# Sparse attention in a hybrid decoder layer: the last 16 queries' index scores packed over heads, the value up-projection in 64-column products, table loads issued by SyncE, weights split in quarters

## What is computed

```python
# index scores: 8 heads of 64, one key for all heads
score = einsum("bqh,bqhs->bqs", wb, relu(einsum("bqhd,bsd->bqhs", qib, ki)))
_, idx = top_k(score, 128)                # among the keys not later than the query
logits = einsum("bqhc,bqkc->bhqk", qb, kv_sel) + bias      # 16 heads, latent width 128
o_lat = einsum("bhqk,bqkc->bqhc", softmax(logits), kv_sel)
o = einsum("bthc,hcd->bthd", o_lat, w_dsa_uv)              # value up-projection, 64 columns a head
```

## Time and profile before

| | us |
|---|---|
| Median of the runs (1400.37 to 1403.15) | 1402.95 |
| Profiled execution, its own time | 1399.39 |
| Its span on the core | 1397.6 |
| TensorE busy | 1331.5 (95%) |
| POOL busy | 791.4 (57%) |
| VectorE busy | 646.8 (46%) |
| ScalarE busy | 389.9 (28%) |

### The profile page before, as it was taken

The page is one execution under the profiler, slowest core; times in us unless marked ns, Lnnn a source line. Parts: engine busy times, 40 slices in busy tenths (PEclk is TensorE's granted clock), DMA queues, the critical chain, the costliest instruction groups (busy, mean ns, idle before and its releaser), DMA issues.

```text
span 1397.6 us, 17236 instructions
## 1 busy us (share of the span) xinstructions
PE 1331.5 (95%) x6467; PEld 1049.4 (75%) x6467; DVE 646.8 (46%) x1111; ACT 389.9 (28%) x789; POOL 791.4 (57%) x919
## 2 busy tenths in 40 slices
PE   6999999989999999999999889999989999999997
PEld 4866787656898778677887567678868888888886
DVE  3248896832246747542365655334252111333334
ACT  4244444443013232333022331331331111211322
POOL 8457433102663544555763553478477777888882
PEclk9999999999999999999999999999989999999999
DMA  6863222101321212222332331252223333222221
GB/s 180 207 218 98 61 61 70 32 22 41 96 76 46 76 46 61 61 61 64 102 85 76 91 91 28 72 181 94 73 80 101 91 91 107 96 99 91 91 91 60
DMA packets 168521, 121.08 MB, mean 87 GB/s; under 512 B 12345, under 2 KB 146591, under 8 KB 168439
## 3 DMA queue, kind: packets, MB, share of 16 engines
q1 hardware_dynamic: 161142, 108.30, 26.5%
q10 hardware_dynamic: 7296, 11.69, 2.8%
HBM read 115.72 MB, written 9.62 MB: 90 GB/s over the span
## 4 chain that ended last, share of the span: by engine, by line
PE 85%; DVE 8%; ACT 3%; issue 2%; ACTq 1%; DMA 0%; DVEq 0%; SPq 0%
PE GP L1671 41%; PE PA L1707 8%; PE GP L1707 6%; PE GP L1686 6%; PE GP L1668 4%; PE PA L1906 3%; PE GP L1857 2%; PE PA L1814 2%; PE PA L1904 1%; PE PA L1837 1%; PE PA L1893 1%; PE PA L1793 1%; PE PA L1870 1%; DVE hres L1596 1%; DVE xn L1595 1%
## 5 line engine op out<-in xcount | busy, mean ns | idle before, releaser
L588 POOL TENSOR_TENSOR wlo<-wraw,whi 128x256 fp32r<-128x256 f32 x712 | 587.0, 854 | 14.8
L584 POOL TENSOR_SCALAR whi<-wraw 128x1024 fp32r<-128x1024 f32 x178 | 195.0, 1096 | 538.1 <-PE GP L1671 319.4
L1671 PE MATMUL GP<-xh,whi 128*128 128x512 f32 x368 | 154.8, 421 | 2.6 <-DVE xl L1151 1.4
L1671 PE MATMUL GP<-xl,whi 128*128 128x512 f32 x368 | 147.7, 401 | 0.0
L1671 PE MATMUL GP<-xh,wlo 128*128 128x512 f32 x368 | 147.7, 401 | 0.0
L1624 DVE TENSOR_TENSOR ul<-U,uh 128x512 fp32r<-128x512 f32 x64 | 65.3, 1058 | 106.8 <-ACT uh L1081 106.8
L1671 PE MATMUL GP<-nh,whi 128*128 128x512 f32 x256 | 102.3, 400 | 0.7 <-DVE nl L1608 0.7
L1671 PE MATMUL GP<-nl,whi 128*128 128x512 f32 x256 | 102.1, 399 | 0.0
L1671 PE MATMUL GP<-nh,wlo 128*128 128x512 f32 x256 | 102.0, 398 | 0.0
L1628 DVE TENSOR_TENSOR U<-U 128x512 f32<-128x512 f32 x32 | 34.6, 1080 | 144.9 <-ACT U L1085 144.9
L1671 PEld LDWEIGHTS GP<-xh,whi 128*128 128x128 f32 x368 | 70.8, 192 | 21.9 <-issue 3.1
(11 more groups left out here) (345 smaller groups left out, 2772.4 us busy)
## 6 DMA issues: line engine op xcount, KB each, us to landing
wraw<-in_w_in SPq DMA_DIRECT2D x75, 512.0 KB, 3.7
wraw<-in_w_up SPq DMA_DIRECT2D x32, 512.0 KB, 4.0
wraw<-in_w_down SPq DMA_DIRECT2D x32, 512.0 KB, 3.5
line_rows<-bias_line SPq DMA_DIRECT2D x1, 5240.0 KB, 26.2
table<-line_rows SPq DMA_DIRECT2D x1, 4096.0 KB, 14.5
wraw<-in_w_br_dsa SPq DMA_DIRECT2D x8, 512.0 KB, 4.7
wraw<-in_w_br_gla SPq DMA_DIRECT2D x8, 512.0 KB, 3.9
wraw<-in_w_br_ml SPq DMA_DIRECT2D x8, 512.0 KB, 4.0
```

The lines of the kernel that those rows point to most:

```text
L584: nc.gpsimd.tensor_scalar(hi, src, 1.0, 1.0, ALU.mult, ALU.mult).then_inc(hi_done, 1)
L588: part = nc.gpsimd.tensor_tensor(lo[:, at:to], src[:, at:to], hi[:, at:to].bitcast(FP32), ALU.subtract)
L1671: ins = mm(ps[0:t.m, 0:SEQ], wt[:, s0, w], av, start=st, stop=sp_)
```

## The change

- The last tile's eight score steps go. The 16 queries of the eight heads are packed in one block of 128 columns (q4, block diagonal over the two halves of 64 rows), one product gives 128 rows (head, query) by 528 keys; VectorE applies relu and the head's weight in one operation, and a product with a 0/1 matrix (selT) adds the heads up. Small operations before the steps prepare the weights by row (wcol) and selT; POOL clears q4.
- SCORE_FILL is rewritten for 24 steps, the query tiles follow after single steps from v = 10 to 14. Between the packed product and the sum stands uq0.
- Eight fewer top-k items are done beside the steps; `rest` has 52 items instead of 44, and `ranked_after` gives two a group up to g = 19, then four in three groups.
- The first half of gb2 moves from group 0 to before the loop.
- The 16 table4 loads and the uvp load move to SyncE, ahead of the load of yb5's chunk, each behind its wait. uvp has 64 columns a head, is not cleared, and comes in one DMA.
- The up-projection writes each head's 64 columns as a product of its own, the first to PSUM partitions 0 to 63, the second to 64 to 127.
- POOL's first pass over a chunk is split in four of 256 columns, as the second is.

```diff
-SCORE_FILL = {1: ["uq4"], 3: ["uq5"], 5: ["uq6"], 7: ["uq7"], 9: ["uq8", "mo0"], 11: ["uq9"], 13: ["uq10"], 15: ["uq11"],
-              17: ["uq12", "mo1"], 19: ["uq13"], 21: ["uq14"], 23: ["uq15"], 25: ["mo2"], 29: ["mo3"]}
+SCORE_FILL = {1: ["uq4"], 3: ["uq5"], 5: ["uq6"], 7: ["uq7"], 9: ["uq8", "mo0"], 10: ["uq9"], 11: ["uq10"], 12: ["uq11"],
+              13: ["uq12"], 14: ["uq13"], 15: ["uq14", "mo1"], 17: ["uq15"], 19: ["mo2"], 21: ["mo3"]}
+LAST_QUERIES = [0, 1, 2, 3]
 GROUP_FILL = ["gb2", "gb3", "gb4", "gb5", "gb6", "gb7", "mo4", "mo5", "mo6", "mo7"]
...
             query(int(name[2:])) if name[:2] == "uq" else gate(name)
-    for h in range(4):
+    for h in LAST_QUERIES:
         query(h)
...
         SO = QO + DSA_H * SEQ * 4
-        (uvp,) = region(SO, [("uvp", [P, DSA_H, P], FP32)])
+        (uvp,) = region(SO, [("uvp", [P, DSA_H, 64], FP32)])
...
         hold_out, ld_mo, mo_sig = sem("hold_out"), sem("ld_mo"), sem("mo_sig")
+        q4_zero, q4i_ok, wc_ps, sc_w, s4_ok = sem("q4_zero"), sem("q4i_ok"), sem("wc_ps"), sem("sc_w"), sem("s4_ok")
         q4_ok, tail_in, gb_sig = sem("q4_ok"), sem("tail_in"), sem("gb_sig")
...
         pt_ps, pt_a, pt_d, pv_ps, ol_ev = sem("pt_ps"), sem("pt_a"), sem("pt_d"), sem("pv_ps"), sem("ol_ev")
-        uv_zero, ld_uv, uv_ps, yh_b, yl_b = sem("uv_zero"), sem("ld_uv"), sem("uv_ps"), sem("yh_b"), sem("yl_b")
+        ld_uv, uv_ps, yh_b, yl_b = sem("ld_uv"), sem("uv_ps"), sem("yh_b"), sem("yl_b")
         ld_a, gla_c, gg_a, gg_l, G_ok = sem("ld_a"), sem("gla_consts"), sem("gg_a"), sem("gg_l"), sem("G_ok")
...
         ROUNDS = TOPK // 8 + 1
+        STEPS = (QT - 1) * IDX_H
+        hmask, hpick, wcol, selT = psm[:, 0:IDX_H], low[:, 0:IDX_H], low[:, IDX_H:IDX_H + 1], prec[:, 0:META]
         WIO = 960
+        WCO = 1000
         GROUPS = QT * NHEADS2 + 1
...
                     sp.wait_ge(split_done, c["r"] - NRAW + 1)
+                if c is chunks[tl["yb5"].chunks[0]]:
+
+                    sp.wait_ge(lg_mn, 3 * DSA_H + 3)
+                    for h_ in range(DSA_H):
+                        sp.dma_start(table4[META * (h_ % 8):META * (h_ % 8 + 1), h_ // 8, :],
+                                     bass.AP(tensor=scratch.tensor, offset=h_ * LPITCH + META - 1,
+                                             ap=[[DSA_H * LPITCH - 1, META], [1, ALL]])).then_inc(tail_in, 16)
+                    sp.wait_ge(keep_ok, QT)
+                    sp.dma_start(uvp[:, :, :], a["w_dsa_uv"][0].rearrange("h c d -> c h d")).then_inc(ld_uv, 16)
...
             nc.gpsimd.memset(lm[:, :, :], 1.0).then_inc(pool_c, 1)
+            nc.gpsimd.memset(q4[:, :, :], 0.0).then_inc(q4_zero, 1)
             pool.wait_ge(pool_c, 7)
...
                                   ident[0:META, 0:META].unsqueeze(1).broadcast_to([META, IDX_H, META])).then_inc(masks, 1)
+            pool.wait_ge(q4_zero, 1)
+            nc.gpsimd.tensor_copy(q4[0:META, 1, :].rearrange("p (h q) -> p h q", q=META),
+                                  ident[0:META, 0:META].unsqueeze(1).broadcast_to([META, IDX_H, META])).then_inc(q4_zero, 1)
             pool.wait_ge(masks, 3 + len(LEVELS))
...
                 src, hi, lo = wraw[:, c["raw"], 0:n], whi[:, c["hl"], 0:n], wlo[:, c["hl"], 0:n]
-                if c is chunks[tl["yb4"].chunks[0]]:
-
-                    pool.wait_ge(keep_ok, QT)
-                    nc.gpsimd.memset(uvp[:, :, :], 0.0).then_inc(uv_zero, 1)
                 pool.wait_ge(raw_in[c["raw"]], c["load"])
...
                     pool.wait_ge(gemm_done, c["after"])
-                nc.gpsimd.tensor_scalar(hi, src, 1.0, 1.0, ALU.mult, ALU.mult).then_inc(hi_done, 1)
+                for at in range(0, n, PIECE):
+                    to = min(at + PIECE, n)
+                    part = nc.gpsimd.tensor_scalar(hi[:, at:to], src[:, at:to], 1.0, 1.0, ALU.mult, ALU.mult)
+                part.then_inc(hi_done, 1)
                 pool.wait_ge(hi_done, c["r"] + 1)
...
                 nc.scalar.activation(qi[:, m, :], ready(f"iq{m}")[:, 0:SEQ], ACT.Copy, scale=0.125).then_inc(gfree[tl[f"iq{m}"].slot], 1)
-            for v in range(QT * IDX_H):
+            act.wait_ge(q4_zero, 2)
+            for m in range(4):
+                whole(f"iq{m}")
+            for e in range(2):
+                r = slice(64 * e, 64 * e + 64)
+                nc.scalar.activation(q4[r, 0, r].rearrange("p (m q) -> p m q", q=META), qi[r, :, TILE_AT[QT]:SEQ], ACT.Copy).then_inc(q4i_ok, 1)
+            for v in range(STEPS):
                 r, w = TILE_ROWS[1 + v // IDX_H], TILE_KEYS[1 + v // IDX_H]
...
                         hold_away(int(name[2:]))
-            act.wait_ge(sc_ps, QT * IDX_H)
-            for h in range(4):
+            act.wait_ge(sc_ps, STEPS + 2)
+            nc.scalar.activation(S[0:META, QT - 1, :], PA[1][0:META, 0:ALL], ACT.Copy).then_inc(s4_ok, 1)
+            act.wait_ge(q4i_ok, 2)
+            for h in LAST_QUERIES:
                 query(h)
...
                                          ACT.Copy).then_inc(ol_ev, 1)
-                if g == 3 * NHEADS2 + 1:
-
-                    act.wait_ge(lg_mn, 3 * DSA_H + 3)
-                    for h_ in range(DSA_H):
-                        act.dma_start(table4[META * (h_ % 8):META * (h_ % 8 + 1), h_ // 8, :],
-                                      bass.AP(tensor=scratch.tensor, offset=h_ * LPITCH + META - 1,
-                                              ap=[[DSA_H * LPITCH - 1, META], [1, ALL]])).then_inc(tail_in, 16)
-                if g == TAIL - 2:
-                    act.wait_ge(uv_zero, 1)
-                    act.dma_start(uvp[:, 0::2, 0:64], a["w_dsa_uv"][0, 0::2].rearrange("h c d -> c h d")).then_inc(ld_uv, 16)
-                    act.dma_start(uvp[:, 1::2, 64:P], a["w_dsa_uv"][0, 1::2].rearrange("h c d -> c h d")).then_inc(ld_uv, 16)
             for m in range(KT):
...
                     if r == 0:
+                        if i == QT:
+                            dve.wait_ge(s4_ok, 1)
                         seq(tt(S[0:n_, i - 1, own], S[0:n_, i - 1, own], later_neg[0:n_, META:META + n_], ALU.add))
...
-            beside = [(1, r) for r in range(ROUNDS)] + [(2, r) for r in range((QT - 1) * IDX_H - ROUNDS)]
-            for v in range(QT * IDX_H):
+            per_head = ident[:, :].rearrange("p (g q) -> p g q", q=META)
+            nc.vector.tensor_reduce(hmask, per_head, mybir.AxisListType.X, ALU.add)
+            seq(nc.vector.tensor_reduce(selT, per_head.rearrange("p g q -> p q g"), mybir.AxisListType.X, ALU.add))
+            dve.wait_ge(wc_ps, 1)
+            seq(tt(hpick, PA[1][:, WCO:WCO + IDX_H], hmask, ALU.mult))
+            seq(nc.vector.tensor_reduce(wcol, hpick, mybir.AxisListType.X, ALU.add))
+
+            ahead = STEPS - IDX_H
+            for v in range(STEPS):
                 i, h = 1 + v // IDX_H, v % IDX_H
...
                 if v >= IDX_H:
-                    tile_, r = beside[v - IDX_H]
-                    dve.wait_ge(sc_acc, tile_ * IDX_H)
-                    topk(tile_, [r])
-            dve.wait_ge(sc_acc, QT * IDX_H)
+                    dve.wait_ge(sc_acc, IDX_H)
+                    topk(1, [v - IDX_H])
+            dve.wait_ge(sc_acc, STEPS)
+            dve.wait_ge(sc_ps, STEPS + 1)
+            ts(rl[:, 0, :], PA[0][:, 0:ALL], 0.0, wcol, ALU.max, ALU.mult).then_inc(sc_w, 1)
             dve.wait_ge(table_in, 16)
...
-            rest = [(2, r) for r in range((QT - 1) * IDX_H - ROUNDS, ROUNDS)] + [(t, r) for t in (3, 4) for r in range(ROUNDS)]
+            rest = [(1, r) for r in range(ahead, ROUNDS)] + [(t, r) for t in (2, 3, 4) for r in range(ROUNDS)]
...
-                return 2 * g if g < 16 else 32 + g - 16
+                return 2 * g if g < 20 else 40 + (g - 20) * 4 // 3
...
                 evacuated(f"iq{m}")
-            for v in range(QT * IDX_H):
+            pe.wait_ge(q4_zero, 2)
+            mm(PA[1][:, WCO:WCO + IDX_H], q4[0:META, 1, :],
+               wi[0:META, QT - 1, :].rearrange("p (m e) -> p e m", e=2), start=True, stop=True).then_inc(wc_ps, 1)
+            for v in range(STEPS):
                 i, h = 1 + v // IDX_H, v % IDX_H
...
                     gemm(name)
-            for h in range(4):
+            pe.wait_ge(q4i_ok, 2)
+            pe.wait_ge(sc_rl, STEPS - 1)
+            for c in (slice(0, SEQ), slice(SEQ, ALL)):
+                ins = mm(PA[0][:, c], q4[:, 0, :], kn[:, c], start=True, stop=True)
+            ins.then_inc(sc_ps, 1)
+            gemm(f"uq{LAST_QUERIES[0]}")
+            pe.wait_ge(sc_w, 1)
+            pe.wait_ge(sc_rl, STEPS)
+            for c in (slice(0, SEQ), slice(SEQ, ALL)):
+                ins = mm(PA[1][0:META, c], selT, rl[:, 0, c], start=True, stop=True)
+            ins.then_inc(sc_ps, 1)
+
+            for h in LAST_QUERIES[1:]:
                 gemm(f"uq{h}")
-
             evacuated(*[f"uq{h}" for h in range(DSA_H)])
-            pe.wait_ge(sc_rl, QT * IDX_H)
             pe.wait_ge(masks, 3 + len(LEVELS))
...
                 logits(v)
```

(8 more changed lines are left out.)

## The result

The changed kernel takes 1377.76 us (median of 4 runs, 1375.82 to 1380.14) against 1401.66 for the kernel before in the same session: a ratio of 0.983 (95% interval 0.9808 to 0.9853), 23.9 us less. The forecast was 14.9 less, 1388.0, and its range ended at 1381. The sign was right, the size was not, and the profiles say where. The profiled execution of after took 1379.02 us, with a span of 1377.1.

The account below looks back on a forecast made before the run. The prediction took TensorE's queue of matrix products to bound the kernel (85% of the span). Its terms summed to -14.9 us, 1384.5 for the profiled execution's kind and 1388.0 for the median, range 1381 to 1397.

Parts of the forecast that it names:

- Split in quarters: POOL's first pass, all 178 chunks: shorter holds of VectorE outweigh POOL's added time, net -2.0 us, bounds +2 to -5.
- Score stage: Packed last-tile scores: eight steps saved, but extra visits, end waits and the selT sum cost more, +1.2 us.
- Start of the loop: Attention loop start: half of gb2 fills TensorE's softmax wait (-1.0) and the half-clock dip goes (-1.5).
- Table loads: Attention group 25: TensorE's stall behind ScalarE's DMA issues goes, -8.2 us; uvp issues leaving ScalarE, -0.3.
- VectorE late next: Attention groups 20 to 28: more top-k items make TensorE wait 0.06 and 0.88 us, +0.9, bounds 0 to +4.
- the cover for yb5's and yb6's weights on SP: SP's queue: table issues take at most 7.5 us, and 50 us cover the weight loads behind them.
- Up-projection: Value up-projection: 64-column products overlap in pairs, 9.5 us against 13.5, -4.0 us, bounds -4.6 and +1.
- the three terms of the packing: Score stage, loop start and later VectorE work: +1.2, -2.5 and +0.9 us.
- Rival (a): Value up-projection: the 64-column products don't overlap, kernel at 1392 us; chance 0.2.
- "some ten" held operations: VectorE's chain, 400 to 1030 us: operations held 0.3 to 0.8 us, halved or better by quarters, -2.5 us.
- Rival (c): Whole kernel lands low: another half-clock stretch moves away with the shift, quarters free 3.5 us more, 1383 us; chance 0.1.
- (d): Last chunks: costlier quarters make POOL the bound, +36 us, 1424; chance 0.04, shared with late weights on SP.

Follow-up runs that it names:

- e2: The changed kernel with POOL's first pass whole again, all other parts kept: 1391.95 us, ratio 0.9938 to the kernel before.
- e3: The kernel before with only the sixteen table loads and two uvp loads moved to SP: 1391.41 us, ratio 0.9937.
- e5: The kernel before with only the value up-projection in 64-column products, uvp in one DMA without clearing: 1395.13 us, ratio 0.9976.
- e9: The kernel before with POOL's first pass in quarters for chunks 76 to 103 only: 1386.38 us, ratio 0.9912.
- e13: The kernel before with eleven unread TensorE products in the waits for the scores of mLSTM heads 1 to 3: 1392.51 us, ratio 0.9923.
- e1: The kernel before with only POOL's first pass cut in quarters, for all chunks: 1386.05 us, ratio 0.9901.
- e10: The kernel before with POOL's first pass in quarters for all chunks but 76 to 103: 1396.75 us, ratio 0.9989.

## Why the prediction was wrong, point by point

The forecast was 14.9 us and the gain 23.9, and the step that failed is the price of the split in quarters, -2.0 against -13.9. The sum hides how large that miss is: the other parts together (e2) gave 8.7 us (5.7 to 11.8) where 12.9 was forecast, so two errors of opposite sign cancel in part.

- **Score stage** (+1.2): +1.95; the two waits at its end, 0.77 and 1.34 us, were sized at 0.6 each, 0.9 us too small together. **Start of the loop** (-2.5): -2.5.
- **Table loads** (-8.2 - 0.3): e3 has -8.5 at the up-projection and -8.8 in all. Right, and so was the cover for yb5's and yb6's weights on SP, though the issues took 8.56 us there and not 7.5.
- **VectorE late next** (+0.9): two waits, 0.86 and 0.73 us, where 0.06 and 0.88 were laid out; with them, the changed kernel's up-projection starts 2.1 us later than that of the loads alone, where the three terms of the packing added up to -0.4. A miss inside its bounds.
- **Up-projection** (-4.0): 9.37 us instead of 13.4; -3.4 (e5). Rival (a) is out: column halves overlap. The Trainium skill, "TensorE: Matmul & The Clock Gate", Part 3, has weight loads overlap running products only where the row groups differ, by which the prediction would have had 4.0 us more. The trace doesn't agree: the two products of a pair share all rows, and eight passes took 1.94 us (at 311.20 us).
- **Split in quarters** (-2.0, bounds +2 to -5): the step that failed. It measured -13.9 alone, 12 us past the term and 9 past its bound. Two assumptions were wrong. The first is the count and the place: "some ten" held operations, of which "a quarter holds for half of that or less". The price was taken from one line of GLA and never from mLSTM's changes of head, where one chain of VectorE operations ends a wait of TensorE four times; 7 us of waits go there (e9), and no row of it stood under the prediction. The second: a shorter wait was priced as its own length. In the kernel before, the half clock behind three of these waits was worth 3.1 us a time, and filling them gained 10.8 us in all (e13, interval 6.9 to 14.7); of this the quarters bring back some 5 (e9). Its cost was missing a place too: POOL makes TensorE wait 3.2 us near 70 us (e1), where only the wait at 998 us was priced, at +0.5; that one stayed at 0.4. Rival (c), with a chance of 0.1, named "another stretch at half clock moves away", but blamed the shift in time for it, at 1.5 us a piece; here one costs 3.1, and it goes with the wait. That it was on the list at all doesn't make the mechanism foreseen.
- **POOL as the bound** (d): its "+36 us" adds up to 32 from its own terms (0.9 x 32 and 0.45 x 32, less 11). In the last stage a quarter takes 0.63 us, past both of the forecast's points (0.48 and 0.6), yet TensorE never waits for POOL there; in e1's trace POOL itself still waits 0.28 us a chunk, where the forecast had 0.3. The second pass got shorter by nearly what the first got longer: 743 ns a piece instead of 927. These are the groups of POOL in the last stage of after, to be read against the 1.05 and 3.60 us of the earlier trace rows:

```profile
L605 POOL TENSOR_TENSOR wlo<-wraw,whi 128x256 fp32r<-128x256 f32 x107 | 76.0, 743 | 2.2
L600 POOL TENSOR_SCALAR whi<-wraw 128x256 fp32r<-128x256 f32 x104 | 62.3, 626 | 7.1 <-PE PA L1731 3.8 <-PE GP L1731 3.3
```

## What to carry to other kernels

When two engines hold one another up, find the places where the held one alone feeds the bound engine, and price the hold there, per operation and per repetition, not from a typical line elsewhere. The held engine's busy time is no measure: here 37 of the 42 us that it lost in e9 and e10 counted for almost nothing. Then look at the granted clock right behind each wait of the bound engine: if it falls there, the wait costs its length and the slow products behind it, and a shorter wait can give back part of both. Cutting a helper engine's operations into pieces is cheap where it has idle time, and costs the bound engine where it has none: cut by stage, not everywhere.

## What the runs showed of the hardware

- Which engine loses when VectorE and POOL work side by side changed with the length of POOL's operation: beside a whole first pass of 1.06 us VectorE's pair took 2.35 us and POOL lost nothing (818 us, before); beside quarters the pair took 1.55 and POOL's 1.6 us became 3.33 (815 us, e1).
- Two 64-column products on disjoint column halves run at once: 8 passes of 512 columns in 1.94 us.
- Work that nobody reads made the kernel 10.8 us faster (6.9 to 14.7): with it the clock stayed at 2.4 GHz behind waits of 4.9 and 2.8 us (1.00 instead of 0.83), and fell at a third place in the same run.
- How often the clock falls varies between executions of the same code: in one session the kernel before took 1395.04 us at a mean clock of 0.983 and 1403.95 at 0.978. So a single profile doesn't price a term of the clock.
